# A forward state-space sweep reordered: masks of both row halves first, 64-row products alternating, value products between, decay sums on GpSimd

## The reference, cut to what matters

```python
acs = cumsum(dt * a)                                  # per head, inside the chunk
decay = exp(where(lower, acs[t] - acs[s], -inf))      # 128 x 128 per head
cb = einsum('bctgn,bcsgn->bctsg', cc, bc)             # 128 x 128 per group
y_diag = einsum('...', cb * decay, xdt)               # the products with the values
y_off = einsum('...', cc, s_in, exp(acs))             # what the state carried in adds
state = state * exp(acs[last]) + st                   # st: what this chunk adds
```

## Time and profile before

| | us |
|---|---|
| median of 3 runs | 2864.4 (2863.81 to 2864.73) |
| the profiled execution, its own time | 2862.88 |
| its span in the trace | 2861.1 |
| TensorE busy over the span | 2707.4 (95%) |
| VectorE busy | 1666.9 (58%) |
| ScalarE busy | 609.7 (21%) |
| GpSimd busy | 983.4 (34%) |

### The profile page before, as it was taken

One profiled execution on the slowest core, in us unless ns is written; L12 is line 12 of the kernel. 1 busy time (PEld: TensorE's weight loads), 2 busy tenths in 40 slices (PEclk: granted clock), 3 DMA queues, 4 the chain that ended last, 5 costly groups with the idle time before them and its releaser, 6 DMA issues. The chain is left out here.

```text
span 2861.1 us, 32418 instructions
## 1 busy us (share of the span) xinstructions
PE 2707.4 (95%) x12452; PEld 2167.2 (76%) x12452; DVE 1666.9 (58%) x2225; ACT 609.7 (21%) x902; POOL 983.4 (34%) x515
## 2 busy tenths in 40 slices
PE   7899999999999999997888999989989999999997
PEld 5688877778888888865676776568767888888885
DVE  8877545756556665686746985963375222222247
ACT  4232232311110011132332103722131110001111
POOL 2122225553333333451212332013545333333343
PEclk9899999999999999998899999999999999999998
DMA  3111132323222322232001343241332111111123
GB/s 138 38 51 44 50 136 83 99 81 102 90 88 88 103 95 82 95 96 75 26 30 41 101 124 121 100 177 44 110 96 85 52 48 44 51 44 51 44 74 103
DMA packets 88484, 228.88 MB, mean 80 GB/s; under 512 B 27520, under 2 KB 30720, under 8 KB 88384
## 3 DMA queue, kind: packets, MB, share of 16 engines
q1 hardware_dynamic: 52384, 172.81, 18.5%
q10 hardware_dynamic: 36000, 54.69, 6.1%
HBM read 197.98 MB, written 28.31 MB: 79 GB/s over the span
## 5 line engine op out<-in xcount | busy, mean ns | idle before, releaser
L195 POOL CAST w_hi<-w_raw 128x1024 fp32r<-128x1024 f32 x254 | 281.8, 1109 | 1813.0 <-PE ps L208 1801.9
L204 PE MATMUL ps<-a_hi,w_hi 128*128 128x512 f32 x2080 | 693.1, 401 | 47.4 <-POOL w_lo L197 18.4
L197 POOL TENSOR_TENSOR w_lo<-w_raw,w_hi 128x1024 fp32r<-128x1024 f32 x254 | 698.7, 2751 | 20.3
L206 PE MATMUL ps<-a_lo,w_hi 128*128 128x512 f32 x2080 | 676.8, 393 | 0.0
L208 PE MATMUL ps<-a_hi,w_lo 128*128 128x512 f32 x2080 | 674.2, 392 | 0.0
L204 PEld LDWEIGHTS ps<-a_hi,w_hi 128*128 128x128 f32 x2080 | 390.3, 191 | 141.4 <-issue 32.7
L206 PEld LDWEIGHTS ps<-a_lo,w_hi 128*128 128x128 f32 x2080 | 395.2, 190 | 83.5
L208 PEld LDWEIGHTS ps<-a_hi,w_lo 128*128 128x128 f32 x2080 | 393.9, 189 | 84.5
L206 PE MATMUL ps<-g_b,w_hi 128*128 128x512 f32 x1216 | 419.2, 396 | 0.0
L204 PE MATMUL ps<-g_b,w_hi 128*128 128x512 f32 x1088 | 369.7, 397 | 9.9 <-DVE g_b L1770 9.9
L208 PE MATMUL ps<-g_b,w_lo 128*128 128x512 f32 x1088 | 368.5, 396 | 0.0
(11 more groups left out here) (451 smaller groups left out, 2748.4 us busy)
## 6 DMA issues: line engine op xcount, KB each, us to landing
w_raw<-in_wstream SPq DMA_DIRECT2D x254, 512.0 KB, 3.5
ada_w<-in_ada_w ACTq DMA_DIRECT2D x25, 512.0 KB, 3.5
ada_w_m<-in_ada_w ACTq DMA_DIRECT2D x25, 512.0 KB, 3.4
y_by_token<-y ACTq DMA_DIRECT2D x12, 512.0 KB, 3.1
x_res_b<-in_xT SPq DMA_DIRECT2D x2, 2048.0 KB, 11.6
x_block<-x_res_b SPq DMA_DIRECT2D x16, 256.0 KB, 3.7
z_rows<-ada_w ACTq DMA_DIRECT2D x8, 512.0 KB, 2.7
u_rows<-pad ACTq DMA_DIRECT2D x8, 512.0 KB, 4.2
```

What stands on the lines that cost most here:

```text
L195: pool.tensor_copy(k.w_hi[:, s, :], k.w_raw[:, s, :]).then_inc(k.w_high, 1)
L197: pool.tensor_tensor(k.w_lo[:, s, :], k.w_raw[:, s, :], k.w_hi[:, s, :].bitcast(F32), ALU.subtract).then_inc(k.w_split, 1)
L204: pe.matmul(o, w_hi, a_hi[:, c], start=first, stop=False)
L206: pe.matmul(o, w_hi, a_lo[:, c], start=False, stop=False)
```

## The change

On TensorE the exponents are issued per group instead of per block: the masks of both directions (4 products of 128 rows), then the four 64-row products with the two row halves alternating. `exponents(i + 1, 0)` stays behind `st`. Then come the wait for `fore_ready` and 6 of the 16 value products, `exponents(i + 1, 1)`, 4 more value products, `cb` of the next chunk, and the last 6. The sum of the two directions' decays moves from VectorE to GpSimd, behind its last weight split, with the same operands. ScalarE's list is not edited.

```diff
@@ gpsimd
             stream_split(pool, k, XBC_END + 2, UZ_END + 2)
+            for i in range(NC):
+                for g in range(NGRP):
+                    pool.wait_ge(s["e_ready"], EXPS * i + 2 * g + 2)
+                    pool.tensor_tensor(big[:, 2 * g, :], big[:, 2 * g, :], big[:, 2 * g + 1, :], ALU.add)\
+                        .then_inc(s["e_sum"], 1)
@@ tensor
-            def exponents(i):
-                pe.wait_ge(s["moving_ready"], i + 1)
-                for j in range(EXPS):
-                    g, r, use = j // 2, j % 2, EXPS * i + j
+            def exponents(i, g):
+                if g == 0:
+                    pe.wait_ge(s["moving_ready"], i + 1)
+                    if i:
+                        pe.wait_ge(s["cb_ready"], i)
+                banks = [k.ps[:, m, :].rearrange("p (h t) -> p h t", t=P) for m in range(4)]
+                for r in range(2):
+                    use = EXPS * i + 2 * g + r
                     if use >= 2:
                         pe.wait_ge(s["e_ready"], use - 1)
...
+                    for b in range(2):
+                        pe.matmul(banks[2 * r + b], ident_r, bc(masks[r], 1, HPG // 2), start=True, stop=False)
+                for b in range(2):
+                    at = g * HPG + b * HPG // 2
+                    for r in range(2):
+                        rows = slice(r * P // 2, (r + 1) * P // 2)
+                        ins = pe.matmul(banks[2 * r + b], v.l_rows[rows, here(i)], moving[rows, at:at + HPG // 2, :],
+                                        start=False, stop=True)
+                        if b == 1:
+                            ins.then_inc(s["d_done"], 1)
...
                 if i + 1 < NC:
-                    exponents(i + 1)
+                    exponents(i + 1, 0)
+                pe.wait_ge(s["fore_ready"], i + 1)
+                diagonal(0, 6)
+                if i + 1 < NC:
+                    exponents(i + 1, 1)
+                diagonal(6, 10)
+                if i + 1 < NC:
                     products_cb(i + 1)
-                pe.wait_ge(s["fore_ready"], i + 1)
-                for h in range(SSM_HEADS):
...
+                diagonal(10, SSM_HEADS).then_inc(s["diag_done"], 1)
@@ vector
-            def add_decays(i):
-                for g in range(NGRP):
-                    dve.wait_ge(s["e_ready"], EXPS * i + 2 * g + 2)
-                    tt(big[:, 2 * g, :], big[:, 2 * g, :], big[:, 2 * g + 1, :], ALU.add).then_inc(s["e_sum"], 1)
...
             for i in range(NC):
-                add_decays(i)
                 if i:
                     last_sum(i - 1)
```

More of the change, by code:

```diff
@@ L2458, in forward, with diagonal @@
                 ins.then_inc(s["st_done"], 1)
-                if i + 1 < NC:
-                    exponents(i + 1)
-                    products_cb(i + 1)
-                pe.wait_ge(s["fore_ready"], i + 1)
-                for h in range(SSM_HEADS):
[L2464 to L2469, removed]
+                def diagonal(h0, h1):
+                    for h in range(h0, h1):
+                        g, cols = h // HPG, slice(h % HPG * P, (h % HPG + 1) * P)
+                        if h % HPG == 0:
+                            pe.wait_ge(s["w_ready"], 2 * i + g + 1)
+                        ins = pe.matmul(Xf[y_at][:, h * HDIM:(h + 1) * HDIM], weights[g][:, cols],
+                                        v.tok[:, i, VAL + h * HDIM:VAL + (h + 1) * HDIM], start=True, stop=True)
+                    return ins
+                if i + 1 < NC:
+                    exponents(i + 1, 0)
[5 more added lines that the diff above has]
+                if i + 1 < NC:
+                    products_cb(i + 1)
+                diagonal(10, SSM_HEADS).then_inc(s["diag_done"], 1)
             for q in range(2):
                 pe.wait_ge(k.pair_free[q], UZ_END // 2)
-            exponents(0)
+            for g in range(NGRP):
+                exponents(0, g)
             products_cb(0)
```

## The result

| | before | changed |
|---|---|---|
| median | 2864.11 us (4 runs) | 2885.13 us (2879.22 to 2885.61, 4 runs) |
| ratio | | 1.0075, 95% interval 1.0062 to 1.0089 |
| span of the profiled execution | 2861.1 us | 2883.8 us |
| granted clock over the span | 0.978 | 0.969 |

The kernel is 21 us slower; 2880 was forecast. A second measurement, beside other kernels, gave 2891.28 against 2862.41, a ratio of 1.0095 (1.0080 to 1.0111). The two medians put the loss at 21 and 29 us, their intervals overlap, and I read both as one result.

The account below looks back on a forecast made before the run. ScalarE's and VectorE's lists were both taken as bounds, within 0.3 us. Start +2.6, longer circle +9.7, exit -0.3 and lowered clock +3.6 made +15.6 us: 2880 for the median, range 2870 to 2893 (81 in 100).

Parts of the forecast that it names:

- The circle: In the sweep, `a_hi`, `a_lo`, VectorE's work, six value products, group 1, exponentials, activations, next `a_hi`: 15.96 us instead of 13.53.
- the lowered clock: TensorE's waits of about 3.6 us in chunks 0 to 5; half lower the clock: +3.6 us, bounds 0 and 10.
- a clock below 0.9 in the sweep: Sign named in advance that would make right the rival in which TensorE stays at the lower clock.
- the third rival: TensorE stays at the lower clock over each chunk's value products, group 1 and `cb`: 2900 us; 9 in 100.
- The moved group lengthens ScalarE's circle: Third and fourth exponentials now wait for group 1 behind `fore_ready` and six value products: four turns 63.8 against 54.12, +9.7 us.
- The signs: Among them: `a_hi` every 16 us in chunks 0 to 4, VectorE idle near 3.8 us before `a_lo`, TensorE 3 to 4.
- Start and exit: Sweep's start up to the first `a_hi` +2.6 us; from the last `a_hi` to the last value products -0.3 us.
- The rest of the kernel: Behind the sweep, the next block of code starts for all engines together; the sweep's loss or gain passes on whole.
- Decay sums on GpSimd: Each sum takes 2.35 us (3.32 kept) and stops VectorE's `weights`; no cost in turns with `a_hi`, three exposed sums otherwise.
- The block of exponents: TensorE's group of four masks and four 64-row products: 2.0 us instead of 2.64, bounds 1.6 and 2.6 to 3.0.
- The sum 4 us lower: If different tiles load and multiply in parallel, a group takes 1.6 us and the forecast falls some 4 us.
- The rival that VectorE bounds: VectorE was the bound and is relieved, 11 to 9 operations per chunk: 17 us faster, 2847; 6 in 100.

Follow-up runs that it names:

- more mask products: Against the full change, each mask product of group 0 done four times in chunks 1 to 7: 2884.62 us, ratio 1.0088; again 2885.54 us, 1.0076.
- the one edit that opens it: Against the full change, ScalarE rounds `a_hi` right behind the copy of `cb`, ahead of the 16 activations: 2863.88 us, ratio 1.0008 to the kernel before.
- order only: Against the full change, the decay sums put back on VectorE, TensorE's new order kept: 2884.86 us, ratio 1.0086 to the kernel before.
- the two kernels with the new order and `a_hi` early: `a_hi` moved ahead of the 16 activations in the full change (2863.88 us, 1.0008) and with the sums back on VectorE (2865.98 us, 1.0010).
- one kernel: Against the full change, groups in their old places with the new block form, sums on VectorE, `a_hi` ahead of the activations: 2882.45 us, 1.0063.

## Why the prediction was right, and where it was off

The forecast of 2880 was 5 us low and the range held the time. The circle came as forecast; the lowered clock did not. By the prediction's own sign, a clock below 0.9 in the sweep, the third rival (9 in 100) was right in that point, and 0.80 was measured; its price, 2900, was too high. Forecast and rival differ only in how long the clock stays low, and the truth lay between them. That the range held is in part luck: the clock cost more than its upper bound (below), and the room of the other terms covered it. The circle step by step:

| step, us | forecast | full change, from 1784.53 | more mask products, from 1817.54 |
|---|---|---|---|
| `a_hi` to the value products | 5.76 | 5.76 | 5.77 |
| to the third exponential (TensorE) | 3.43 | 5.38 | 3.22 |
| to the activations (`cb` between) | 2.09 | 3.14 | 2.11 |
| to the next `a_hi` | 4.68 | 4.67 | 4.67 |
| turn | 15.96 | 18.95 | 15.77 |

The first and the last step, VectorE's and ScalarE's, came within 0.01 us of the forecast. The whole excess of the full change lies in the two steps that hold TensorE's work, and it is gone where the clock is 1.00.

- **The moved group lengthens ScalarE's circle**: right. Forecast 15.96 us a turn, four turns +9.7; with the clock kept up, four turns are 64.5, +10.4. That it is this circle is shown by the one edit that opens it, which brings the full change's ratio from 1.0075 and 1.0095 to 1.0008 (on one chip, 2863.88 us with the edit beside 2884.86 for order only without it), and by order only being as slow as the whole. The signs were smaller than forecast: VectorE waited 3.52 or 2.35 us before `a_lo`, not 3.8.
- **The clock**: the mis-sized term. I took three spells at 1.2 us, +3.6. In the turns it cost 8.5 at least, and it was low again from chunk 7's value products on: they took 5.53 us for 3.79, and the next block of code came 13.97 us after their start, not 10.73. That is 3.2 more, and together 11.7, outside the bounds of 0 to 10. The step that failed is the reading of the earlier trace rows as one lowered stretch of 3.4 us for every second spell: the stretches here lasted up to 16.8 us, and the sweep's mean of 0.80 over 133.5 us means 53 us at the half clock. The 3.2 at the end belong less surely to the change: order only did not have them (10.74), and the two kernels with the new order and `a_hi` early did (13.93 and 13.94).
- **Start and exit**: forecast +2.6 and -0.3, measured +2.2 and +0.5.
- **The rest of the kernel**, which I passed on whole, gave back 2.1. Over the kernels profiled here it varied between 980.6 and 988.9 us without an edit in it.
- **Decay sums on GpSimd**: that they cost nothing in the turns held in the new order, where VectorE waits for `a_hi` anyway (order only is no faster). I had them stop `weights` alone; by themselves they cost 6.9 us, since they stop VectorE's work on the output, the state and the weighed values too.
- **The block of exponents**: taken at 2.0 us, it is 1.8: four masks with the change between them 1.14, four 64-row products 0.66 with the change out. That four such products cost what two did, and start in pairs 4 ns apart, agrees with the Trainium skill's page "TensorEngine Tiling (Array Packing)", section Key Properties, that different tiles can run in parallel. The sum 4 us lower, which I set beside it, would have been further off, as the clock outweighs it. But I had not priced the other side of the form: with all four banks taken, group 1 waits for two exponentials instead of one.
- **The rival that VectorE bounds**: its operations do bound the kernel before once `a_hi` is early (12.76 us without a gap). The 13.4 us that I gave them was too much, as they overlap a little. They were the second bound, 0.5 us under ScalarE's circle of 13.22. Moving the sums off VectorE alone made the kernel slower; but as GpSimd stops VectorE, no run shows what a real relief would give.

What stays open: which idle pattern lowers the clock. Single spells of 1.97 us before the change did not, nor one of 2.74; three short ones within four microseconds were followed by a drop in some chunks of one kernel and not in others. No experiment varied the spells alone.

## What to carry to other kernels

Before moving a block behind a new wait, follow the whole list of the engine that consumes it: what stands last in that list comes late by the same amount, and if the wait depends on it, the delay is paid every turn. Look for the short operation that closes such a circle, here 1 us of rounding behind 4.7 us of activations, for which TensorE waited 2.0 us in the whole sweep before, and move that one: it was worth 5.5 us, where a larger reshuffle lost 21. And before giving VectorE's work to GpSimd, look at what VectorE does meanwhile: here its operations with two SBUF operands took up to 3.40 us beside a sum, where they take 1.22.

## What the runs showed of the hardware that I had not expected

- More work made the sweep shorter: 12 more mask products a chunk in TensorE's wait raised its clock in the sweep from 0.80 to 0.97 and shortened four turns by 8.5 us (5.7 us in the medians of one chip).
- The clock fell amid spells of 1.11, 0.20 and 1.11 us (0.57 over the 16 us from 1791), where one spell of 1.97 or 2.74 us before the change had left it at 1.00; the same three spells later in that kernel left it at 1.00 too (1850.58 to 1864.42).
- Once low, the clock stayed at 0.50 for 13.4 us with TensorE busy all the time, and in another stretch for 16.8 us.
- Two 64-row products between masks took 0.66 us, and four of them also 0.66, alternating or half by half: in either order they start in pairs, one of each half.
- The 16 decay sums on GpSimd took 2.35 us at the shortest, 3.44 at the longest and 2.59 on the mean; VectorE's state operation met by one took 3.39 instead of 1.22.
